# A decoder trunk's SBUF tiles placed anew: small tiles first, the large ones at multiples of 2 KB

## What is computed

```
for l in range(2):
    h = adaLN(rmsnorm(x), c)
    z = h @ w_in[l]                       # 1024 -> 4640 columns
    ya, yb, yc = spatial_gating(z), latent_attention(z), multi_scale_pool(z)
    merged = sum of sigmoid(gate_i) * (y_i @ w_i[l])
    x = x + g1 * (merged @ w_o[l])
    h2 = adaLN(rmsnorm(x), c)
    # experts: 8 heads, 16 of 16,384 experts each, found by product keys
    a = gelu(u_tab[eidx] . h2);  g = softmax(top scores)
    x = x + g2 * sum over chosen experts of (g * a) * v_tab[eidx]
x = rmsnorm(x) * final_norm
```

## Time and profile before

| | |
|---|---|
| median of 3 runs | 3514.66 us (3512.41 to 3514.79) |
| profiled execution, first to last instruction (its span) | 3511.6 us |
| what the median has above that span | 3.1 us |
| TensorE matmul busy | 98% |
| VectorE, ScalarE, POOL busy | 69%, 40%, 39% |
| moved by DMA | 910 MB, mean 259 GB/s |

### The profile page before, as it was taken

The page is one execution under the profiler, slowest core; times in us unless marked ns, Lnnn a source line. Parts: engine busy times, 40 slices in busy tenths (PEclk is TensorE's granted clock), DMA queues, the critical chain, the costliest instruction groups (busy, mean ns, idle before and its releaser), DMA issues.

```text
span 3511.6 us, 53302 instructions
## 1 busy us (share of the span) xinstructions
PE 3448.3 (98%) x17974; PEld 2925.7 (83%) x17974; DVE 2418.7 (69%) x4725; ACT 1400.6 (40%) x2298; POOL 1372.5 (39%) x1291
## 2 busy tenths in 40 slices
PE   7999999999999999999999999999999999999999
PEld 5776799999999877777777777999999998777777
DVE  6455679999887865555464566899998868555554
ACT  3334244343576332332333333434346753332232
POOL 1011108667743434444400110277668325344442
PEclk9999999999999999999999999999999999999999
DMA  6375447776899989999735743577779999899995
GB/s 239 118 257 183 144 135 228 215 226 189 263 344 324 387 304 350 353 354 348 297 128 178 229 149 130 189 220 207 208 226 278 345 337 368 313 359 350 357 350 185
DMA packets 306403, 910.04 MB, mean 259 GB/s; under 512 B 69076, under 2 KB 101892, under 8 KB 305316
## 3 DMA queue, kind: packets, MB, share of 16 engines
q0 software_dynamic: 163792, 473.58, 39.8%
q1 hardware_dynamic: 105552, 383.83, 31.6%
q10 hardware_dynamic: 36868, 50.35, 3.9%
HBM read 792.14 MB, written 115.47 MB: 258 GB/s over the span
## 4 chain that ended last, share of the span: by engine, by line
PE 90%; DVE 3%; DMA 2%; POOL 2%; issue 2%; ACT 1%; ACTq 0%; SPq 0%; DVEq 0%; POOLq 0%
PE ps L461 15%; PE ps L463 14%; PE ps L462 14%; PE ps L1078 10%; PE ps L1080 10%; PE ps L1079 10%; PE ps L1092 3%; PE ps L1058 3%; PE ps L881 2%; PE ps L978 1%; PE ps L937 1%; PE ps L979 1%; PE ps L980 1%; PE ps L1018 1%; POOL weight_spill L757 1%
## 5 line engine op out<-in xcount | busy, mean ns | idle before, releaser
L461 PE MATMUL ps<-mov,whl 128*128 128x384 f32 (+1 forms) x2816 | 1007.1, 358 | 1.1 <-DVE whl L448 1.1
L463 PE MATMUL ps<-mov,whl 128*128 128x384 f32 (+1 forms) x2816 | 986.7, 350 | 0.0
L462 PE MATMUL ps<-mov,whl 128*128 128x384 f32 (+1 forms) x2816 | 986.1, 350 | 0.0
L448 DVE TENSOR_TENSOR whl<-raw,whl 128x1024 fp32r<-128x1024 f32 x648 | 793.5, 1225 | 220.1 <-ACT whl L438 215.6
L438 ACT CAST whl<-raw 128x1024 fp32r<-128x1024 f32 x648 | 679.7, 1049 | 102.6 <-ACT hst L1273 96.4
L1078 PE MATMUL ps<-whl,wgthl 128*128 128x512 f32 x1536 | 611.3, 398 | 3.4 <-DVE wgthl L1817 3.3
L1080 PE MATMUL ps<-whl,wgthl 128*128 128x512 f32 x1536 | 609.1, 397 | 0.0
L1079 PE MATMUL ps<-whl,wgthl 128*128 128x512 f32 x1536 | 603.8, 393 | 0.0
L461 PEld LDWEIGHTS ps<-mov,whl 128*128 128x128 f32 x2816 | 529.7, 188 | 39.1 <-issue 8.7
L463 PEld LDWEIGHTS ps<-mov,whl 128*128 128x128 f32 x2816 | 529.0, 188 | 31.5
L462 PEld LDWEIGHTS ps<-mov,whl 128*128 128x128 f32 x2816 | 529.9, 188 | 30.2 <-issue 2.2
(11 more groups left out here) (271 smaller groups left out, 3645.5 us busy)
## 6 DMA issues: line engine op xcount, KB each, us to landing
raw<-in_uT_tab SPq DMA_DIRECT2D x256, 512.0 KB, 4.1
raw<-in_v_tab SPq DMA_DIRECT2D x256, 512.0 KB, 6.9
expert_spill<-hst ACTq DMA_DIRECT2D x256, 192.0 KB
hin<-expert_spill POOLq DMA_DIRECT2D x256, 192.0 KB, 7.3
gt<-weight_spill POOLq DMA_DIRECT2D x64, 768.0 KB, 8.6
raw<-in_w_in SPq DMA_DIRECT2D x72, 512.0 KB, 5.4
raw<-in_w_mod SPq DMA_DIRECT2D x64, 512.0 KB, 3.6
weight_spill<-stage POOLq DMA_DIRECT2D x14, 2048.0 KB, 13.3
```

What stands on the lines that cost most here:

```text
L448: nc.vector.tensor_tensor(whl[:, m % RING, 1], raw[:, raw_n(m) % RAW], whl[:, m % RING, 0].bitcast(F32), ALU.subtract).then_inc(lo_done, 1)
L461: nc.tensor.matmul(o, w[:, 0, k], src[:, 0, k, :cols], start=(k == 0), stop=False)
L462: nc.tensor.matmul(o, w[:, 0, k], src[:, 1, k, :cols], start=False, stop=False)
L463: mm = nc.tensor.matmul(o, w[:, 1, k], src[:, 0, k, :cols], start=False, stop=(k == KC - 1))
```

## The change

The allocator rounds the start of each tile of 512 bytes or more up to a multiple of 64 (`LINE`). The tiles up to `root`, with `kr` and `wpl`, come first. Then `x_sb` starts at a multiple of 2,048 (`ROW`), with `mov`, `raw` and `whl` behind it, whose sizes are multiples of 2,048, too. The stage tiles begin at `free`, which is rounded up to `ROW`, so `mrg` and `qT` start there; `wgthl` gets a `ROW` of its own. `rt`, the rope's scratch, now lies on `root`, and VectorE waits for the last latent norm before it first writes there. Nothing else is edited: no instruction is added or taken away but that wait, and none changes its shape. The diff, cut to its core (what is left out are more `on_line()` calls of the same kind and the moved lines as they stood):

```diff
+LINE, ROW = 64, 2048
...
-    top_of = [nc.sbuf_base + -nc.sbuf_base % 32]
+    top_of = [nc.sbuf_base + -nc.sbuf_base % 64]
+
+    def on_line(line=LINE):
+
+        top_of[0] += -top_of[0] % line
+        return top_of[0]
...
-        off = top_of[0] if at is None else at
+        line = LINE if size >= 8 * LINE else 32
+        off = top_of[0] + -top_of[0] % line if at is None else at
         if at is None:
-            top_of[0] += size
+            top_of[0] = off + size
...
-    x_sb = sb("x_sb", [P, KC, S])
-    mov_at = top_of[0]
-    mov = sb("mov", [P, 2, KC, S], F32R)
-    vrow = sb("vrow", [P, VR, D], at=mov_at)
-    raw = sb("raw", [P, RAW, KC, P])
-    whl = sb("whl", [P, RING, 2, KC, P], F32R)
     mod = sb("mod_cols", [P, N_MOD])
...
-    sq_at = top_of[0]
+    sq_at = on_line()
     sq = sb("sq", [P, 2, S])
+    root_at = top_of[0]
     root = sb("root", [P, S])
-    free = top_of[0]
-    assert sq_at + 4 * 4 * SD <= free
+    kr = sb("kr", [P, TT, ROPE])
+    wpl = sb("wpl", [P, 2, 64])
+    on_line(ROW)
+    x_at = top_of[0]
+    x_sb = sb("x_sb", [P, KC, S])
+    mov_at = on_line()
+    mov = sb("mov", [P, 2, KC, S], F32R)
+    vrow = sb("vrow", [P, VR, D], at=mov_at)
+    raw = sb("raw", [P, RAW, KC, P])
+    whl = sb("whl", [P, RING, 2, KC, P], F32R)
+    free = on_line(ROW)
+    assert sq_at + 4 * 4 * SD <= x_at
...
-    kr = sb("kr", [P, TT, ROPE])
-    rt = sb("rt", [P, 4, HEADS, HALF])
+    rt = sb("rt", [P, 4, HEADS, HALF], at=root_at)
...
     wgt = sb("wgt", [P, 2, SD])
+    on_line(ROW)
     wgthl = sb("wgthl", [P, 2, 2, SD], F32R)
...
                     if i == 0:
                         dve.wait_ge(rope_made, 2)
+                        dve.wait_ge(lat_norm, l * 5 + 5)
```

More of the change, by code:

```diff
@@ L242, in build_trunk @@
     ones = sb("ones", [P, P])
-    causal_at = top_of[0]
+    causal_at = on_line()
     causal = sb("causal", [P, P])
@@ L276, in build_trunk @@
     vh = sb("vh", [P, TT, HEADS * VD])
-    y_at = top_of[0]
+    y_at = on_line()
     y = sb("y", [P, KC, S])
@@ L280, in build_trunk @@
     tok = sb("tok", [P, 2, HEADS, QK], at=y_at + 8192)
-    lat_at = top_of[0]
+    lat_at = on_line()
     lat = sb("lat", [P, 5, S])
@@ L285, in build_trunk @@
     band = sb("band", [P, 12, P], at=lat_at + 4096)
-    gst_at = top_of[0]
+    gst_at = on_line()
     gst = sb("gst", [P, 6, S])
     uq = sb("uq", [P, 3, HEADS * QK], at=gst_at)
-    kr = sb("kr", [P, TT, ROPE])
-    rt = sb("rt", [P, 4, HEADS, HALF])
+    rt = sb("rt", [P, 4, HEADS, HALF], at=root_at)
     ug = sb("ug", [P, 2, S])
-    pv_at = top_of[0]
+    pv_at = on_line()
     vg = sb("vg", [P, TT, 2 * P])
@@ L296, in build_trunk @@
     prT = sb("prT", [P, 4, S], at=lat_at)
-    wpl = sb("wpl", [P, 2, 64])
-    ht_at = top_of[0]
+    ht_at = on_line()
     ytmp = sb("ytmp", [P, 2, S])
@@ L318, in build_trunk @@
     idv = sb("idv", [P, QUADS, QT], U32)
-    htok_at = top_of[0]
+    htok_at = on_line()
     htok = sb("htok", [P, D])
@@ L326, in build_trunk @@
     hin = sb("hin", [P, 4, SD], at=sq_at)
-    pick_at = top_of[0]
+    pick_at = on_line()
     qh = sb("qh", [P, 2, S])
@@ L343, in build_trunk @@
     stage = sb("stage", [P, 2, P, TB])
-    hot_at = top_of[0]
+    hot_at = on_line()
     hot2 = sb("hot2", [P, 2, GT, P])
```

## The result

The changed kernel takes 3483.0 us (median of 4 runs, 3480.4 to 3485.7) against 3514.7 before (4 runs, 3512.4 to 3521.5). The ratio is 0.9909, with a 95% interval of 0.9895 to 0.9923. The forecast was 3483.

What follows compares the result with a forecast made beforehand. TensorE's matmul spacing was taken as the bound. Weighing's 29.0 us plus `mrg`'s 2.5 made 31.5 us, so 3511.6 - 31.5 + 3.1 = 3483 us, range 3386 to 3518.

Steps and rivals of the forecast that it cites:

- What bounds the kernel: TensorE, busy 98% of the span and 90% of the chain: what counts is how closely its matmuls follow each other.
- The reading of the three addresses: `mrg` and `wgthl` start 32 past a multiple of 64, `mov` and `whl` on one; off a line costs one 6.67 ns step.
- (1): Weighing of expert rows: 4,608 matmuls from 233.3 to 226.7 ns save 30.4 us, less 1.4 at 34 restarts, net 29.0.
- (2): Matmuls that stream `mrg`: 384 x 6.6 ns, 2.5 us saved, also on the path.
- (3): `mov`, `raw`, `whl`, `x_sb` shift by -128 bytes modulo 2,048 and start at a line now and then: 0.
- (4) to (6): VectorE and ScalarE accesses, true f32 matmuls, and VectorE's added wait before the first rope product: each taken as 0.
- (7): Transfers: faster weighing raises the DMA share to 0.91 to 0.92; they still fit and nothing is late.
- Rival B: No measurable change: the weighing's 6.6 ns is not the address, only (2) stays, 3512 us; chance 0.14.
- Rival C: A boundary of 256 or 512 bytes counts: 3294 us if both remaining steps go, 3390 if one; chance 0.18.
- Rival D: Slower: `wgthl` and `whl` starting at the same place of 2,048 bytes make the weighing 240 ns, 3543 us; chance 0.10.
- A: The forecast itself: one 64-byte step less where an operand was off a line, 3478 to 3488 us; chance 0.58.

Runs made afterwards that it cites:

- run 1: The kernel before with `wgthl` alone pushed on by 32 bytes, to 64 past a multiple of 2,048: 3501.1 us, ratio 0.9957.
- run 4: The changed kernel with `mov`, `whl`, `mrg` and `wgthl` all 32 bytes off a line of 64, at unequal distances: 3519.0 us, ratio 1.0018.
- run 5: The changed kernel with `mov`, `whl`, `mrg` and `wgthl` all 32 past a multiple of 512, so at distance 0: 3483.7 us, ratio 0.9906.
- run 10: The changed kernel with the weighing's hi x lo matmul loading 64 stationary columns in place of 128: 3496.1 us, one execution.
- run 11: The changed kernel with stream-to-stationary distances modulo 256 of 16 bytes in weighing and panels, 240 with `mrg`: 3503.8 us, one execution.

## Why the prediction was right, and where its reason was wrong

- **What bounds the kernel.** Right. TensorE stayed 98% busy, and the interval in the weighing decided the result.
- **The reading of the three addresses.** Wrong, and it is the step that failed: "I read the third step as one 64-byte piece more, which an operand touches when it starts in the middle of one." Runs 1 and 4 contradict it from both sides (all on lines: 228.6; all off lines: 228.6 to 229.2), run 5 settles it (off lines, distance 0: 226.8 to 227.0). The near clean comparison of `mrg` with `mov` changed two things at once, the place modulo 64 and the distance to `whl`, and the prediction saw only the first. The match of 13.2 and 19.8 ns with two and three times 6.67 was chance: 64 and 128 give 228.6 and 232.1, on no such step.
- **(1) Weighing.** 4,608 x 6.62 = 30.5 us of shorter intervals, against 30.4 in the sum. The size was right because it was read from the best and the worst pair in the trace and the change did move one to the other. The loss of 1.4 us at 34 restarts was charged too high: it was read from a start of the `mov` stream, as if a restart of the weighing cost nothing at 233.3 ns. It costs 0.104 us over nine steps before and 0.130 after, which leaves some 0.9 us. What the sum did not have is the wait for `wgthl`, which grew by 1.9 us. The stages shortened by 27.1 against 29.0 in the sum.
- **(2) `mrg`.** 6.6 ns per matmul as forecast, but the stage with its norm kept nothing: the term of 2.5 us for both layers came to 0.3 us of loss, and it went with the norm's longer time at 1.2 GHz. The prediction put it "also on the path" and did not ask what follows it.
- **The total.** That 3483 was met to the microsecond is luck. The weighing and `mrg` brought 26.8 us of the 31.5 in the sum; the rest of the 30.8 that the span lost came from stretches that the sum had at 0, the largest piece of it a wait for `hotg` in the kernel before.
- **(3) `mov`, `raw`, `whl`, `x_sb`.** 0 was right, and the sentence held the true reason without using it: "`mov` and `whl` keep their distance". The panels kept 227.2 ns at 512 columns, and at 384 went from 173.8 to 173.5.
- **(4) to (6).** VectorE's subtraction takes 1,223 ns where it took 1,225. The expert weights' true f32 matmuls start 1.7 / 15 = 113 ns apart as before. The rope waits for ScalarE as before. All as forecast.
- **(7) Transfers.** The shares are 0.91 and 0.90, and none of TensorE's larger waits is for a transfer: as forecast.
- **Rival B.** Its mechanism, that the place within a line does not matter, was half true; its time was wrong, since the address does matter. The Trainium skill's "SBUF — State Buffer", Specifications, has lines of 16 bytes, by which nothing would have changed. The runs disagree: starts at multiples of 32 span 226.7 to 233.9 ns, with a period of 256.
- **Rival C.** A boundary of 256 does count, but for the difference of two starts; the panels were already at 0, so nothing more was to be had there, and its 3,294 and 3,390 us could not come.
- **Rival D.** It named the right quantity, the distance of `whl` and `wgthl`, and the wrong sign. The row that I set against it ("share such a place today ... shortest distance in the trace") was the rule itself.

So a chance of 0.58 on A rested on a reason that one run of the kernel before could not separate from its rival. Had the change only put `wgthl` on a line of 64, as in run 1, the same reason would have forecast 3,484 to 3,488 us and been 13 to 17 us out.

What is shown is the table. Why the distance acts is not: run 10, where a shorter load made the matmuls slower, and run 11 fit a picture in which the load of the next block and the running stream meet in the same part of the memory at some offsets and not at others, but no run shows the memory itself. Nor do the runs tell whose block counts: every block and chunk lies a multiple of 512 bytes from its tile's start, so the block in use and the one loaded next have the same distance.

## What to carry to other kernels

When a pair of tiles feeds TensorE back to back, with another stationary block for each f32r matmul as here, compare the start-to-start interval for each pair and write beside it the difference of the two starts modulo 256; make it 0 (here 226.7 instead of 233.3 ns for 512 columns), which may take one padding of 96 bytes and no new layout. Before a price is put on an address, look for two pairs that differ in one property only: a place and a distance change together when one tile is moved. And where a stage gets shorter in front of a norm, look at the granted clock of the norm before counting the gain.

## What was not expected of the hardware

- The interval of f32r matmuls depends on the distance of the operands' starts modulo 256, in no simple order: 32 and 96 cost 6.6 ns, 64 only 2.
- At 384 columns distances of 64 and 224 cost nothing, where at 512 they cost 2 and 6.6 ns.
- A stationary block of half the columns loads in 134 ns in place of 188 and makes the mean interval 3.5 ns longer (226.7 to 230.2), not shorter.
